# Tokens in two groups: the second half's recurrent chain between the expert slots of the first half's tiles, sums in column halves, and the expert phase unrolled

## What is computed

```
h = x + W_out( concat[A, B, C, D](rmsnorm(x) @ W_in) )
x = h + PEER(rmsnorm(h))         # and a final rmsnorm
  A: conformer convolution: GLU -> causal depthwise conv, width 31 -> layernorm -> swish
  B: RWKV-7 time mixing, 4 heads of 64; for every token, in order:
       sa = einsum('bhij,bhj->bhi', s, -kk)
       s  = s * w + sa * (kk * a) + v * k
       y  = einsum('bhij,bhj->bhi', s, r)
  C: short gated convolution,  D: causal means over 2/4/8/16 positions
PEER, 8 heads, for every token and head:
  q = x @ Wq ; scores of q against two sets of 128 keys ; the best 16 of the
  16 x 16 sums of the best name 16 of 16384 experts, softmax over them gives g
  out += sum over the 16 experts e of  g_e * gelu(u_e . x) * v_e
```

## Time and profile before

| | before |
|---|---|
| median of 3 runs | 1790.93 us (1789.02 to 1792.27) |
| profiled execution, its own time | 1790.03 us |
| its span in the profile | 1788.0 us |
| granted TensorE clock, mean | 0.96 of full speed |
| PE busy | 1524.6 us (85%) |
| DVE busy | 1213.6 us (68%) |
| POOL busy | 848.2 us (47%) |
| ACT busy | 682.9 us (38%) |
| DMA | 580.38 MB, mean 325 GB/s |

### The profile page before, as it was taken

The page is one execution under the profiler, slowest core; times in us unless marked ns, Lnnn a source line. Parts: engine busy times, 40 slices in busy tenths (PEclk is TensorE's granted clock), DMA queues, the critical chain, the costliest instruction groups (busy, mean ns, idle before and its releaser), DMA issues.

```text
span 1788.0 us, 20036 instructions
## 1 busy us (share of the span) xinstructions
PE 1524.6 (85%) x5360; PEld 833.1 (47%) x5360; DVE 1213.6 (68%) x2658; ACT 682.9 (38%) x1920; POOL 848.2 (47%) x1108
## 2 busy tenths in 40 slices
PE   5989799868989889888979897888889798988776
PEld 4878798533354334343534443443434343433221
DVE  2696683572667777676767676777667676777775
ACT  2113322122434444443434444444444344444554
POOL 0001741023447655555546554656555555655552
PEclk9999999989989999999999999999999999999999
DMA  4312212147699999999999999999999999999996
GB/s 133 106 48 65 5 48 83 52 188 238 244 377 412 421 421 421 421 378 422 421 417 380 422 422 378 422 421 422 369 422 421 422 373 422 422 421 421 422 421 261
DMA packets 96684, 580.38 MB, mean 325 GB/s; under 512 B 23888, under 2 KB 24144, under 8 KB 28256
## 3 DMA queue, kind: packets, MB, share of 16 engines
q0 software_dynamic: 74880, 545.29, 74.5%
q1 hardware_dynamic: 21728, 34.26, 6.3%
HBM read 576.33 MB, written 3.19 MB: 324 GB/s over the span
## 4 chain that ended last, share of the span: by engine, by line
issue 36%; POOL 33%; PE 16%; DVE 7%; DMA 5%; ACT 2%; POOLq 1%; DVEq 0%; SPq 0%; ACTq 0%
POOL arena L1652 24%; POOL arena L1651 9%; PE ps L451 5%; DMA arena<-in_uv,arena 4%; PE ps L521 3%; DVE arena L1102 3%; PE ps L762 3%; DVE arena L1096 2%; PE ps L565 1%; POOLq L1649 0%; POOLq L1650 0%; PE ps L711 0%; PE ps L433 0%; PE ps L500 0%; PE ps L693 0%
## 5 line engine op out<-in xcount | busy, mean ns | idle before, releaser
L762 PE MATMUL ps<-arena 128*128 128x512 f32 (+1 forms) x2080 | 1009.8, 624 | 192.5 <-ACT arena L1038 188.7
L1473 DVE CUSTOM_DVE_ANT_0 arena<-arena 128x1024 f32<-128x1024 f32 x520 | 636.7, 1226 | 341.4 <-DMA arena<-in_uv,arena 294.0
L762 PEld LDWEIGHTS ps<-arena 128*128 128x128 f32 (+1 forms) x2080 | 378.1, 194 | 761.7 <-ACT arena L1038 384.2
L1652 POOL DMA_INDIRECT arena<-in_uv,arena x520 | 601.3, 1156 | 84.1 <-POOL arena L1651 16.5
L1651 POOL TENSOR_TENSOR arena<-arena 1x1 f32<-1x1 f32 x520 | 172.6, 332 | 551.5 <-PE ps L762 525.3
L1031 ACT ACTIVATE arena<-arena 128x1 f32<-128x1 f32 x520 | 104.9, 202 | 679.6 <-DVE arena L1473 677.4
L1038 ACT ACTIVATE arena<-arena 128x128 f32<-128x128 f32 (+1 forms) x520 | 208.0, 400 | 70.2 <-PE ps L762 23.4
L1096 DVE TENSOR_TENSOR arena<-arena 128x256 f32<-128x256 f32 (+6 forms) x197 | 127.2, 646 | 48.3 <-ACT arena L866 33.0
L1033 ACT ACTIVATE arena<-arena 128x1 f32<-128x1 f32 x520 | 153.2, 295 | 16.9
L451 PE MATMUL ps<-arena 128*128 128x260 f32 x608 | 139.2, 392 | 1.8 <-ACT arena L935 1.0
L711 PEld LDWEIGHTS ps<-arena 128*128 128x128 f32 x1024 | 127.5, 203 | 26.8 <-issue 17.8
(11 more groups left out here) (147 smaller groups left out, 916.4 us busy)
## 6 DMA issues: line engine op xcount, KB each, us to landing
arena<-in_win SPq DMA_DIRECT2D x19, 512.0 KB, 3.6
arena<-in_wqk SPq DMA_DIRECT2D x8, 1152.0 KB, 9.4
arena<-in_uv,arena POOLq DMA_INDIRECT x520
arena<-in_wout SPq DMA_DIRECT2D x6, 1024.0 KB, 5.6
arena<-in_xp SPq DMA_DIRECT2D x4, 512.0 KB, 7.8
out_yp<-arena SPq DMA_DIRECT2D x4, 512.0 KB
arena<-in_const SPq DMA_DIRECT2D x1, 928.0 KB, 4.7
arena<-in_n SPq DMA_DIRECT2D x1, 512.0 KB, 5.3
```

Source lines behind the costliest of these rows:

```text
L762: last = mm(ps[0:m, b + c, :], diag[:, s % 4, 0:m], ring[:, s % RING, D + 512 * c:D + 512 * c + 512], start=(s == 0), stop=(s == slots - 1))
L1473: v.tensor_tensor_reduce(out=ring[:, s % RING, 0:D], in0=ring[:, s % RING, 0:D], in1=row, scale=1.0, scalar=0.0, op0=MUL, op1=ADD, accum_o ...
L1652: pool.indirect_dma_start(out=ring[:, s % RING, :], out_offset=None, in_=a["uv"][:, :], in_offset=bass.IndirectOffsetOnAxis(ap=idx[:, t, s ...
```

## The change

**Two groups of tokens.** Group 0 is tiles 0 and 1 and the samples (264 columns), group 1 is tiles 2 and 3 (256). `project` becomes `zcol`, one block for one group: 38 of them, in the order `ZORDER`; a block whose two groups don't follow each other is loaded twice, which makes 26 loads of weights for the 19 before. The recurrent work of a group is written on PE, DVE and ACT as a generator `mixer(g)`, whose steps carry a number, the tick. `Steps.until(n)` emits the steps up to tick n. `mixer(0)` is emitted ahead of the slots, with the projection's blocks and the taps of the convolution (now 256 wide, 31 x 2 for each group) between its steps. `mixer(1)` is emitted between the slots: on DVE and ACT `later.until(k)` stands at the end of slot k, on PE behind each pair of slots. The ticks of a group run from 0 to about 142: features 0 to 20, transposes from 22, first products from 31, levels 40 to 79 (8 ticks each), `C_P` from 81, chunks from 86 (6 ticks each), the head norm from 110, output projection, second norm and its transposes from 121.

**Order of the units.** Heads 0 to 5 for tiles 0 and 1; heads 0 to 5 for tiles 2 and 3; heads 6 and 7 for all tiles. Each change of head loads `wqk`: 14 loads for 8.

**Slots.** A slot now covers 64 tokens and two experts of each: the even slot the lower 64 tokens of a tile, the odd one the upper 64 (rows of tokens come doubled in `xpair`, and indices and gates are put in place by `placed`). The diagonal is 128 x 64. PE takes slots in pairs: it waits for the second diagonal of a pair, and then does four matmuls of 512 columns whose outputs lie on PSUM partitions 0 to 63 and 64 to 127. The bytes fetched by a slot are the same.

**Unrolled.** The expert phase has no hardware loop any more on any engine. Six partial products of the output projection for tiles 2, 3 and 4 (36 logical matmuls of 512 columns) stand on PE right ahead of unit 0, and DVE adds them in between the steps of `choose(0)` and `choose(1)`.

The core of the diff:

```diff
-            def project(i):
-                pe.wait_ge(d_w[i % 3], 16 * (i // 3 + 1))
-                if i >= 2:
-                    pe.wait_ge(S["z_copied"], i - 1)
-                for h in range(2):
-                    for k in range(KT):
-                        last = mm(ps[:, 2 * (i % 2) + h, 0:HALF], wring[:, i % 3, k, :], hT[:, k, HALF * h:HALF * h + HALF],
-                                  start=(k == 0), stop=(k == KT - 1))
+UNITS = [(h, t) for h in range(FIRST) for t in (0, 1)] + [(h, t) for h in range(FIRST) for t in (2, 3)] \
+    + [(h, t) for h in range(FIRST, HEADS) for t in range(TILES)]
...
+    def until(self, tick):
+        while not self.ended and self.due <= tick:
+            self.advance()
...
+C_TOK, C_G, C_L1, C_LV, C_P, C_CH, C_LN, C_OUT = 22, 31, 36, 40, 81, 86, 110, 121
@@ SP
-            sp_.wait_ge(S["short_done"], 1)
-            sp_.wait_ge(S["pool_out"], 2)
+            sp_.wait_ge(S["short_done"], 2)
+            sp_.wait_ge(S["pool_out"], 4)
@@ PE, a level of the mixer
+                        yield base
+                        pe.wait_ge(S["lm_ready"], PER["lm_ready"] * g + n_ + 1)
+                        pe.wait_ge(S["tinv_done"], PER["tinv_done"] * g + 2 if lv == 1 else n_ + 1)
+                        if n_:
+                            pe.wait_ge(S["u_copied"], PER["u_copied"] * g + n_)
+                        four(q, 5, lm[g], tinv[g]).then_inc(S["u_mm"], 1)
+                        yield base + 2
...
+                        four(q, 6, u_sb[g], tinvt[g]).then_inc(S["vt_mm"], 1)
+                        yield base + 3
...
+                            four(q, 7, tinvt[g], u_sb[g]).then_inc(S["v_mm"], 1)
@@ PE, slots
-                for s in range(slots):
-                    pe.wait_ge(S["diag_done"], TOPK * u + s + 1)
-                    for c in range(2):
-                        last = mm(ps[0:m, b + c, :], diag[:, s % 4, 0:m], ring[:, s % RING, D + 512 * c:D + 512 * c + 512],
-                                  start=(s == 0), stop=(s == slots - 1))
-                    last.then_inc(S["slot_used"], 1)
+                for s in range(0, TOPK, 2):
+                    pe.wait_ge(S["diag_done"], TOPK * u + s + 2)
+                    for c in range(2):
+                        for q in range(2):
+                            last = mm(ps[64 * q:64 * q + 64, b + c, :], diag[:, (s + q) % 8, :],
+                                      ring[:, (s + q) % RING, D + 512 * c:D + 512 * c + 512],
+                                      start=(s == 0), stop=(s == TOPK - 2))
+                            if c:
+                                last.then_inc(S["slot_used"], 1)
+                    for q in range(2):
+                        if u + LEAD < NU:
+                            prepare(u + LEAD, s + q)
+                        later.until(TOPK * u + s + q)
@@ DVE, a level of the mixer
+                            yield base + 1
+                            dve.wait_ge(S["u_mm"], PER["u_mm"] * g + n_ + 1)
+                            lt_level(g, q, lv + 1).then_inc(S["lm_ready"], 1)
+                            yield base + 4
+                            dve.wait_ge(S["v_mm"], PER["v_mm"] * g + n_ + 1)
+                            tt(tinvt[g][:, u, :], tinvt[g][:, u, :], bank4(6), ADD).then_inc(S["tinvt_done"], 1)
+                            lk(tt(tinv[g][:, u, :], tinv[g][:, u, :], bank4(7), ADD).then_inc(S["tinv_done"], 1))
@@ DVE, slots
-            with dve.Fori(1, HEADS - 1) as h:
-                for t in range(TILES):
-                    unit(h, t, ahead(h, t, LEAD), ahead(h, t, 1))
+            for u in range(NU + 1):
+                unit(u)
```

More of the change, by code:

```diff
@@ L518, in four, with turn_half @@
+            def turn_half(t, half, bank):
+                n = width(t)
+                for k in range(4 * half, 4 * half + 4):
+                    last = turn(ps[:, bank, (k % 4) * 128:(k % 4) * 128 + n], xn2[t][0:n, 128 * k:128 * k + 128], ident[0:n, 0:n])
+                last.then_inc(S["turned2"], 1)
             def four(q, bank, left, right):
@@ new lines, in _ @@
+            for t in (0, 1, TILES):
+                turn_x(t)
+            pe.wait_ge(S["hT_done"], 3)
+            zcol()
+            turn_x(2)
+            zcol()
+            turn_x(3)
+            zcol()
+            first = Steps(mixer(0))
+            for k in range(3):
+                first.until(E_LORA + 2 * k)
+                zcol()
+            zcol()
+            first.until(E_SUM)
+            zcol(4)
+            pe.wait_ge(S["hT_done"], TILES + 1)
+            first.until(E_BONUS)
@@ L997, in queries @@
+            first.until(C_P + 1)
+            zc()
+            sample_copy(0)
+            first.until(C_P + 4)
+            for c in range(GC):
+                if c == 1:
+                    sample_copy(1)
+                zc()
+                first.until(C_CH + 6 * c + 4)
+            conf_root(1)
+            conf_sigmoid(1)
+            first.until(C_LN + 4)
+            first.finish()
+            def queries(v):
                 act.wait_ge(S["q_mm"], v + 1)
-                if not (isinstance(h, int) and v == 0):
+                if v:
@@ new lines, in both, with taps, conf_center @@
+            def both():
+                yield from convolution(0)
+                yield from convolution(1)
+            conv = both()
+            def taps(count):
+                for _ in range(count):
+                    next(conv, None)
+            def conf_center(g):
+                n = GN[g]
+                c, q = cacc[g][:, :, 0:n], csq[:, :, 0:n]
+                dve.wait_ge(S["conf_centered"], g + 1)
+                lk(tt(c, c, ps[:, 2:3, 0:n].to_broadcast([128, 2, n]), SUB))
+                tt(q, c, c, MUL).then_inc(S["conf_sq"], 1)
@@ new lines, in _ @@
+            first.until(C_P + 4)
+            taps(4)
+            for c in range(GC):
+                first.until(C_CH + 6 * c + 1)
+                taps(2)
+                first.until(C_CH + 6 * c + 3)
+                taps(2)
+                if c == 1:
+                    sample_output()
+                    taps(64)
+                if c == 2:
+                    conf_center(1)
+            first.until(C_LN + 2)
+            add_partial(0, 0, 0, 2)
+            conf_scale(1)
+            conf_swish(1)
@@ L1538, in _ @@
-            add_unit(TILES * HEADS, TILES)
+                choose(1, step)
+                if step in (4, 9):
+                    add_partial(6 if step == 4 else 7, 3, int(step == 9), 6 if step == 4 else 7)
+            add_partial(8, 4, 0, 6)
+            add_partial(9, 4, 1, 7)
+            lk(v.memset(sscore[0:64], 0.0))
+            for u in range(NU + 1):
+                unit(u)
+            add_unit(NU)
             final_mean(TILES)
```

2302 lines of the change are left out of this document (1307 added, 995 removed).

## The result

| | before | after |
|---|---|---|
| median | 1791.16 us (1789.02 to 1792.27, 4 runs) | 1975.73 us (1973.75 to 1980.24, 4 runs) |
| ratio | | 1.1034, 95% interval 1.1018 to 1.1051 |
| span of the profiled execution | 1788.0 us | 1974.4 us |
| mean granted clock of TensorE | 0.96 | 0.81 |

The changed kernel is slower by 185 us, over three times the 52 us that I forecast. The sign and the place were right; the size was not, and 1975.7 lies outside the range. One of the prediction's own signs of being wrong came true too: the first dot product is at 367.3, and it was to be before 350.

What follows compares the result with a forecast made beforehand. DMA was taken to set the pace, 2.49 us a slot. 340 + 543 + 919 + 22 + 5 + 19 - 8 = 1840 for the span, 1842 for the execution against 1790.0; range of 8 in 10: 1755 to 1915.

Steps and rivals of the forecast that it cites:

- signs of being wrong: Wrong if DVE's idle time in the first 143 slots is ended by DMA, or first dot not before 350.
- the walk through DVE's own work and its waits at full clock: Slots 0 to 142: mixer ticks counted as dots, steps and waits behind PE, 497 us less 14 for `choose`.
- the clock: Slots 0 to 142: PE at half speed after long idles adds 1.8 us to some 28 of them, +50 us.
- The head: Everything ahead of the slots: first fetch at 311, 61 us earlier, and first dot at about 340 against 393.
- (R4): Rival for the head: output projection's early weights wait for POOL; first fetch at 346, total 1877 us; chance 0.10.
- The rest: From slot 143 on: 919 us at 2.49 a slot, loads 22, output writes 5, tail 19, less 8.
- the formula: The sum of terms for the span's end, with a tail of 19 us from the last byte.
- The 8 us that I took off: Correction to the span's end: the same sum for the kernel before gave 1796, 8 too many.
- The unrolling: Turns of the loop over heads go: six dips of some 4.7 us of DMA lost each, 28 us.
- (R1): Rival for slots 0 to 142: DVE's waits are absorbed, slots take 375 us, total 1674 us; chance 0.15.
- (R2): Rival for slots 0 to 142: waits are there but PE's clock stays full, 493 us, total 1792 us; chance 0.20.
- (R3): Rival for a pair's sums on PE: column halves don't run side by side, total 1915 us; chance 0.13.

Runs made afterwards that it cites:

- e11: The changed kernel with eight added zero-matrix matmuls of 512 columns behind each pair of units 3 and 4 alone: 1964.4 us (one run).
- e6: The changed kernel with four added zero-matrix matmuls of 512 columns behind each pair in units 1 to 8: 1949.6 us.

## Why the prediction was wrong in size, and where it was right

**The mechanism** is the one of the prediction: a step of DVE behind the dot of its slot, a product behind the sums of a pair, the pair behind the second diagonal. With two slots of distance, nothing else changed, the 203 us lost in these slots are back, and 7 more.

**The step that failed in slots 0 to 142** is the walk through DVE's own work and its waits at full clock. Of my 543 us, 50 were for the clock and 10 for table loads, which leaves 483 for this walk. In the trace DVE is busy for 362 of the 607 us and waits behind PE for 223, in 43 waits, as many as I had. The clock is not what I missed. Full clock in those parts of the 43 waits in which PE worked at half clock would have saved 56 us, an estimate from the granted clock and PE's busy times, and I had 50. So the walk should have given 362 + 223 - 56 = 529 for 483, 46 of the 64 us. Another 12 are DVE's idle time for ACT and in small gaps (22 us, where I had 10), and 6 are the clock.

The experiments bear the count of the clock out. By the same count the waits of slots 48 to 80 hold 22 us of it in after and 6 in e11, and e11 is 21 us shorter there; those of all 143 slots hold 56 in after and 35 in e6, and e6 is 25 us shorter. So a microsecond of it may cost 1.2 to 1.4 us of time, which would make it up to some 75 us: at most 25 more than I had. It came out near although more pairs ran at half clock than I thought, 47 and not 28, since only what lies inside a wait costs anything.

My walk had no term for what else stands in a wait. Between the sums of a pair and the product of the mixer PE has the query of the unit two ahead, once in a unit, and its scores; 32 us of this work lie inside the 43 waits. Here it makes a wait of 8.50 us:

```profile
564.00 2.55 PE L972 MATMUL ps<-arena 128*64 128x512 f32 x8 [3.78 <-ACT arena L1270]
566.48 4.84 PE L891 MATMUL ps<-arena 128*128 128x128 f32 x32
571.16 1.06 PE L603 MATMUL ps<-arena 128*128 128x128 f32 x8
572.25 0.69 DVE L1306 TENSOR_TENSOR arena<-arena 128x512 f32<-128x512 f32 x1 [8.50 <-PE ps L603]
```

And a step of the mixer on ACT that waits for PE stands ahead of the gelu of dots that are done: of the 8.31 us of idle time ahead of DVE's step at 698.83, some 2.6 us went by between the end of a dot at 689.8 and its gelu at 692.4, after ACT's own wait had ended at 691.9. Four slots of a level hold 9.2 us of DVE's own work, where I had 7.55; the 40 slots of the levels took 195 us for 155, and the 9 slots of the first products and the first level 58 for 39. No run takes the query or ACT's step out of the waits, so their shares are read from the trace and not tested.

**The head.** The first fetch came at 336.1 and not at 311, the first dot at 367.3 and not at 340. The chunks ended at 263 instead of 249; in them PE stood idle for 6.1 us, up to 236.56, until POOL had done its part of the samples' chain, which I had counted as going on beside them. Then PE stood idle for the early weights of the output projection:

```profile
262.46 1.13 PE L748 MATMUL ps<-arena 128*128 128x256 f32 x4 [0.37 <-ACT arena L1141]
273.06 2.90 PE L584 MATMUL ps<-arena 128*128 128x512 f32 x3 [9.46 <-DMA arena<-in_wout]
```

14 + 9.5 = 24 of the 25 us. (R4) had these weights late for another reason, the short convolution and pools on POOL. But POOL's last operation before them ended at 245.5, and SP issued the loads at 260.0, after it had waited until 248.2 for DVE's sums of the samples and then 10.2 us for its own stores of the tails to land. The distance from the fetch to the first dot held: 29 us forecast, 31.2 measured.

**The rest.** From slot 143 on 1000 us for 957. 20 of the 43 are the tail that the formula did not count, as told above; the others are the pace: 2.62 us a slot between dots 143 and 512 (968.3 / 369), where I had 2.49 plus 27 / 369 = 2.56 with loads and outputs. The 8 us that I took off had the wrong sign: by the prediction's own terms the kernel before comes to 795 + 919 + 14 + 28 + 5 + 19 = 1780, which is 8 too few for its span of 1788.0. The unrolling was worth 9 and not 28 us; that the six more loads of a head's weights (17 us by my 2.8 us each, an estimate) take it back is not tested.

**The rivals.** (R1), 1674 us, waits that are absorbed: not in the changed kernel, but it is what two slots of distance bring about, and even then the total is 1762, because the head (by 25 us), these slots (397 for 375) and the rest (997 for 957) were too good in my sum. (R2), full clock: out, 47 of 71 pairs' sums took over 3 us. (R3), halves one after the other: out. Eight instructions of 64 columns take 1.94 us where PE runs warm, as long as four of 128 columns did:

```profile
498.94 1.94 PE L972 MATMUL ps<-arena 128*64 128x512 f32 x8 [3.85 <-ACT arena L1270]
504.92 1.94 PE L972 MATMUL ps<-arena 128*64 128x512 f32 x8 [2.95 <-ACT arena L1270]
```

With that the rule of the Trainium skill, "TensorE: Matmul & The Clock Gate", Part 3: Packing small matmuls, is borne out by the trace: outputs in distinct column groups run side by side. Its gain was never on the path, though: single slots give it up and win 162 us.

The chances were wrong as well. 0.69 for slower was right, but the range ended at 1915 because I let only one mishap in at a time. Three terms missed on the same side: the slots of the chain by 64 us, the rest by 43, the head by 27.

## What to carry to other kernels

When a chain that goes back and forth between engines is put in the gaps of a loop, the consumer's step belongs some iterations behind the producer's, so that each engine meets results that are ready. Put right behind, it makes each iteration as long as the whole round trip: here no distance, one slot and two slots gave 1976, 1824 and 1762 us with the same instructions. A batch that waits for the last of several inputs (the pair of slots) lengthens that round trip, and it can cost far more than the work that it saves.

## What the runs showed of the hardware that I had not expected

The length of the last idle time did not decide TensorE's clock. In the changed kernel 1.94 us for a pair's sums followed 3.85 us of idle (row above), and 3.68 us an idle time hardly longer:

```profile
485.32 3.68 PE L972 MATMUL ps<-arena 128*64 128x512 f32 x8 [3.94 <-ACT arena L1270]
```

Ahead of the idle time of 3.85 us PE had worked for 9.8 us without a gap, ahead of this one for 4.5. And a kernel whose PE was 60 to 72% busy at the DMA's pace held a clock of only 0.76 to 0.85 from 1000 us on, without any loss of time. Straight code in place of a loop took away 33 us of "issue" idle time ahead of the dots and gave 9 us; I had taken the whole dip of DMA at each turn for a loss that would be won.
